# A gated feed-forward in which each pair of a gate block and an up block is made with seven block products, on one core of a Trainium2

## The reference

```python
def swiglu(x, w_gate, w_up, w_down):
    return (jax.nn.silu(x @ w_gate) * (x @ w_up)) @ w_down

    h = h + 0.5 * swiglu(rmsnorm(h, ffn1_norm[i]), ffn1_w_gate[i], ffn1_w_up[i], ffn1_w_down[i])
    ...
    h = h + 0.5 * swiglu(rmsnorm(h, ffn2_norm[i]), ffn2_w_gate[i], ffn2_w_up[i], ffn2_w_down[i])
    gate = jax.nn.sigmoid(rmsnorm(h, ple_gate_norm[i]) @ ple_w_gate[i])
    emb = rmsnorm(p[i] @ ple_w_proj[i], ple_norm[i])
    h = h + gate * emb
```

## Time and profile before

| | us |
|---|---|
| median of 3 runs | 2253.64 |
| lowest, highest | 2253.39, 2257.74 |
| profiled execution | 2255.11 |
| its span, first to last instruction | 2253.3 |
| PE busy | 2224.9 |
| DVE busy | 1337.6 |
| ACT busy | 892.6 |
| POOL busy | 321.0 |

### The profile page before, as it was taken

How to read it: one execution, slowest core, us unless ns; L and a number is a source line. 1 busy time by engine, 2 the same in 40 slices (tenths; PEclk the granted TensorE clock), 3 DMA queues, 4 the chain that set the end, 5 groups by cost and what they waited for, 6 DMA issues and landing times.

```text
span 2253.3 us, 30491 instructions
## 1 busy us (share of the span) xinstructions
PE 2224.9 (99%) x12660; PEld 1855.0 (82%) x12667; DVE 1337.6 (59%) x1562; ACT 892.6 (40%) x1190; POOL 321.0 (14%) x191
## 2 busy tenths in 40 slices
PE   9999999999999999999999999999999999999999
PEld 7888888878888888888886789899876858898998
DVE  6434446597644345475557675576567874855754
ACT  4222234345422332353238543344434574533532
POOL 2000001030100100021002123123100301231230
PEclk9999999999999999999999999999999999999999
DMA  5233322320233323232320133333333201334332
GB/s 190 94 94 94 111 75 86 101 72 20 84 99 107 93 94 93 76 111 94 113 75 20 55 107 111 122 112 104 99 115 80 72 20 45 115 112 122 106 110 94
DMA packets 201186, 208.12 MB, mean 92 GB/s; under 512 B 7042, under 2 KB 195218, under 8 KB 201076
## 3 DMA queue, kind: packets, MB, share of 16 engines
q1 hardware_dynamic: 201076, 206.56, 29.6%
...
## 4 chain that ended last, share of the span: by engine, by line
PE 91%; DVE 6%; ACT 2%; issue 1%; DMA 0%; SPq 0%; ACTq 0%; DVEq 0%
PE psum L867 78%; PE psum L957 4%; PE psum L955 4%; PE psum L956 4%; DVE sm L2880 1%; DVE w_lo L404 1%; DVE rstd L2287 0%; PE psum L1409 0%; PE psum L1401 0%; DVE free_x L2269 0%; ACT w_hi L391 0%; ACT free_h L1685 0%; DVE free_h L2272 0%; DVE free_x L3002 0%; DVE sm L3000 0%
## 5 line engine op out<-in xcount | busy, mean ns | idle before, releaser
L867 PE MATMUL psum<-xg_lo,w_hi 128*128 128x512 f32 (+1 forms) x1576 | 608.5, 389 | 0.4 <-ACT free_x L1685 0.4
L867 PE MATMUL psum<-xg_hi,w_hi 128*128 128x512 f32 (+1 forms) x1528 | 596.2, 390 | 3.9 <-DVE xg_lo L2269 1.7
L867 PE MATMUL psum<-xg_hi,w_lo 128*128 128x512 f32 (+1 forms) x1528 | 592.9, 388 | 0.0
L391 ACT ACTIVATE w_hi<-w_raw 128x2048 fp32r<-128x2048 f32 (+1 forms) x148 | 281.6, 1903 | 382.9 <-PE psum L867 363.3
L404 DVE TENSOR_TENSOR w_lo<-w_raw,w_hi 128x2048 fp32r<-128x2048 f32 (+1 forms) x146 | 340.9, 2335 | 151.2 <-ACT w_hi L391 148.0
L867 PEld LDWEIGHTS psum<-xg_lo,w_hi 128*128 128x128 f32 x1576 | 295.6, 188 | 62.2 <-ACT free_x L1685 1.4
L867 PEld LDWEIGHTS psum<-xg_hi,w_hi 128*128 128x128 f32 x1528 | 287.0, 188 | 68.0 <-issue 4.9
L867 PEld LDWEIGHTS psum<-xg_hi,w_lo 128*128 128x128 f32 x1528 | 286.9, 188 | 59.5
L867 PE MATMUL psum<-h_hi,w_hi 128*128 128x512 f32 x696 | 278.1, 400 | 3.1 <-DVE w_lo L404 2.8
L867 PE MATMUL psum<-h_hi,w_lo 128*128 128x512 f32 x696 | 271.8, 391 | 0.0
L867 PE MATMUL psum<-h_lo,w_hi 128*128 128x512 f32 x696 | 271.8, 390 | 0.0
...
## 6 DMA issues: line engine op xcount, KB each, us to landing
...
```

Source lines behind the costliest of these rows:

```text
L391: e.activation(w_hi[:, wside(c), 0:n], w_raw[:, c % 2, 0:n], ACT.Copy).then_inc(sem("hi_done"), 1)
L867: return pe.matmul(out, lhsT, rhs, start=start, stop=stop)
```

## The change

The gated feed-forwards join `FAST`. ffn1 keeps two plain pairs at its start, ffn2 one (`PLAIN`); the other 2 + 4 + 3 and 3 + 4 + 3 pairs, 19 in all, are made by `fast_up` on PE and by a new function `fast_gated` on ACT and DVE, with a gate block and an up block as the two weight blocks. POOL's sums are written out for them too. The activation sums of ffn1 are made between its plain pairs, through the buffer `trig` (the sine and cosine tables, which are not in use yet); those of ffn2 are made in wout1, as wout2 does for mlp0. The constants move up in the larger `arena`, the embedding input and its split move into `buf_a`, `buf_b`, `buf_c` and `ssq`, its load comes later, its result moves, its sum and root go into `trig`. In the second group of ffn2 the load of `w_third` waits for the sum of the embedding's squares, since both use `sq`. The scratch memory for GpSimd's own DMAs, which the kernel does not issue, shrinks to make room. The core of the diff:

```diff
-FAST = ("mlp0", "mlp1")
+FAST = ('ffn1', 'ffn2', 'mlp0', 'mlp1')
+PLAIN = {"ffn1": 2, "ffn2": 1, "mlp0": 1, "mlp1": 1}
+STAGE = {"ffn1": 0, "ffn2": 2, "mlp0": 5, "mlp1": 7}
 def plan():
...
         sq = alias("sq", [P, 2, S], F32, 4 * KB + 2 * S * 4)
         rs_hi = alias("rs_hi", [P, S], F32R, 4 * KB + S * 4)
         rs_part = nc.alloc_sbuf_tensor_at("rs_part", [P, 2, P], F32R, offset=buf_d_at)
...
-                first, n_pairs = at[name, g, "up"] + (2 if g == 0 else 0), tiles // per - (g == 0)
+                plain_pairs = PLAIN[name] if g == 0 else 0
+                first, n_pairs = at[name, g, "up"] + 2 * plain_pairs, tiles // per - plain_pairs
+                group_first[name, g] = first
+                if n_pairs % 2:
+                    odd_turn[first] = len(odd_turn)
...
-        X_WITH = {"wout2": ((), (0, 1), (2,), ()), "wout3": ((0,), (1,), (2,), ())}
-
...
+        X_WITH = {"wout1": ((), (0, 1), (2,), ()), "wout2": ((), (0, 1), (2,), ()), "wout3": ((0,), (1,), (2,), ())}
...
+        def x_raw(p, i):
+
+            return trig if p == 0 else (buf_a, buf_c)[i % 2]
...
+
+            def load_p(buffer_free):
+
+                sp.wait_ge(sem("ms"), 3)
+                sp.dma_start(pos_int, io["positions_2"]).then_inc(sem("p_in"), 16)
+                sp.wait_ge(*buffer_free)
+                sp.dma_start(p_raw[:], io["p"].rearrange("(k p) t -> p k t", p=P)).then_inc(sem("p_in"), 16)
...
-                        sp.wait_ge(sem("ssq_done"), 7 * (p + 1))
+                        sp.wait_ge(*(third_free or (sem("ssq_done"), 7 * (p + 1))))
...
+                    if wg is not None and name in FAST:
...
+                        fast_loads(group_first[name, g], p, lambda q: (vu[:, :, (q + ahead) * BC:(q + ahead + 1) * BC],
+                                                                       vg[:, :, (q + ahead) * BC:(q + ahead + 1) * BC]),
+                                   (sem("emb_ssq"), 7) if (name, g) == ("ffn2", 1) else None)
...
+                            if (name, g, i) == ("ffn2", 0, 1):
+                                load_p((sem("u_read"), fast_groups[c0][-1] + 1))
...
-                        fast_up(c + 2 if g == 0 else c, p)
+                        for j in range(1, PLAIN[name] if g == 0 else 0):
+                            blk(c + 2 * j, a=xg(p))
+                            blk(c + 2 * j + 1, a=xg(p))
+                        fast_up(group_first[name, g], p)
...
+                def silu(q):
+                    if q >= 0:
+                        act.wait_ge(sem("gate_scaled"), made[q] + 1)
+                        a(buf_a[:], buf_a[:], ACT.Silu).then_inc(sem("silu"), 1)
+
+                def hidden_hi(q):
+                    if q < 0:
+                        if ahead:
+                            of_plain()
+                        return
+                    t = 2 * (q + ahead)
+                    act.wait_ge(sem("hmul"), h0 + q + 1)
+                    a(hidden(p)[0][:, t:t + 2, :], buf_b[:], ACT.Copy).then_inc(sem("h_hi_done"), 1)
...
+                for q in range(len(made)):
+                    split(7 * q + 3)
+                    silu(q - 1)
+                    copy(q, 0)
+                    split(7 * q + 4)
+                    hidden_hi(q - 1)
+                    copy(q, 1)
+                    split(7 * q + 5)
+                    copy(q, 2)
+                    for n in range(6, 10):
+                        split(7 * q + n)
+                q = len(made) - 1
+                hi(act, after)
+                silu(q)
+                hidden_hi(q)
+                hi(act, after + 1)
...
+                        for j in range(last):
+                            gated_pair(j, first=True)
...
+                            if p == 0:
+                                for i in range(2):
+                                    x_scale(p, i)
+                                    x_high(p, i)
+                                hi(act, c0)
+                            act.wait_ge(sem("evac"), c0 - 1)
+                            a(buf_c[:], buf_a[:], ACT.Silu).then_inc(sem("silu"), 1)
+                            if p == 0:
+                                for i in range(2, 4):
+                                    x_scale(p, i)
+                                    x_high(p, i)
...
+                def last_quarter(q):
+                    if q >= 0:
+                        dve.wait_ge(*strip_mark("pe", c0, 7 * q + 6))
+                        tt(buf_b[:, :, TS:S], by_halves(pair_banks(c0, q)[0]), scale[:, :, TS:S], ALU.mult).then_inc(sem("evac"), 1)
+
+                def gate_up(q):
+                    if q >= 0:
+                        dve.wait_ge(sem("evac"), c0 + 2 * q + 2)
+                        dve.wait_ge(sem("silu"), s0 + q + 1)
+                        tt(buf_b[:], buf_b[:], buf_a[:], ALU.mult).then_inc(sem("hmul"), 1)
...
+                for q, pair in enumerate(made):
+                    run, side_sum, first_sum = pair_banks(c0, q)
+                    last_quarter(q - 1)
+                    split(7 * q + 3)
+                    gate_up(q - 1)
+                    split(7 * q + 4)
+                    hidden_lo(q - 1)
+                    split(7 * q + 5)
+                    split(7 * q + 6)
+                    dve.wait_ge(*strip_mark("pe", c0, 7 * q + 3))
+                    dve.wait_ge(sem("h_done"), h0 + q)
+                    tt(buf_b[:, :, 0:TS], by_halves(first_sum), scale[:, :, 0:TS], ALU.mult)
+                    split(7 * q + 7)
+                    dve.wait_ge(*strip_mark("pe", c0, 7 * q + 4))
+                    tt(buf_a[:, :, TS:S], by_halves(run), by_halves(buf_c[:, q % 2, :]), ALU.add).then_inc(sem("u_read"), 1)
+                    split(7 * q + 8)
...
+                    dve.wait_ge(*strip_mark("pe", c0, 7 * q + 5))
+                    tt(buf_a[:, :, 0:TS], by_halves(side_sum), by_halves(buf_d[:, q % 2, :]), ALU.add).then_inc(sem("evac"), 1)
...
+                    dve.wait_ge(sem("u_read"), pair + 1)
+                    dve.wait_ge(sem("evac"), c0 + 2 * q + 1)
+                    stt(buf_a[:], buf_a[:], -1.0, scale, ALU.mult, ALU.mult).then_inc(sem("gate_scaled"), 1)
+                    split(7 * q + 9)
+                q = len(made) - 1
+                last_quarter(q)
+                gate_up(q)
+                hidden_lo(q)
                 lo(dve, after + 1)
...
+                                    x_split(p, i)
+                                    x_low(p, i)
+                            evac_scaled(c0 - 2, buf_a)
...
+                            if p == 0:
+                                lo(dve, c0)
+                                for i in range(2, 4):
+                                    x_split(p, i)
+                                    x_low(p, i)
+                            evac_scaled(c0 - 1, buf_b)
+                            dve.wait_ge(sem("evac"), c0)
+                            dve.wait_ge(sem("silu"), s0 + ahead)
+                            tt(buf_d[:], buf_b[:], buf_c[:], ALU.mult).then_inc(sem("hmul"), 1)
...
...
                     dve.wait_ge(sem("p_in"), 32)
-                    dve.tensor_copy(pos_row, arena[0:1, 1024:1536].bitcast(I32)).then_inc(sem("pos_f32"), 1)
+                    dve.tensor_copy(pos_row, pos_int).then_inc(sem("pos_f32"), 1)
...
+            def other_sums(c0):
+
+                made = fast_groups[c0]
+                for q, pair in enumerate(made):
+                    c = c0 + 2 * q
+                    pool.wait_ge(sem("w22_in"), 16 * (pair + 1))
+                    pool.wait_ge(*strip_mark("lo", c0, 7 * q + 1))
+                    add_rows(w_run[run_half[pair]], raw22(c0, q), sem("w_next"))
+                    pool.wait_ge(sem("w21_third_in"), 16 * (pair + 1))
+                    add_rows(w_third, raw22(c0, q), sem("w_third"))
+                    if q + 1 < len(made):
+                        first_sum(c0, q + 1)
+                    pool.wait_ge(sem(f"landed{(c + 1) % 2}"), 16 * ((c + 1) // 2 + 1))
+                    pool.wait_ge(*strip_mark("lo", c0, 7 * q + 2))
+                    add_rows(w_run[run_half[pair]], raw(c + 1, 0), sem("w_next"))
+
+            def fast_sums(name, with_first=None):
+
+                for g in range(len(GROUPS[name]) if name in FAST else 0):
+                    c0 = group_first[name, g]
+                    first_sum(c0, 0)
+                    if with_first and g == 1:
+                        with_first()
+                    other_sums(c0)
...
+            fast_sums("ffn1")
...
+            fast_sums("ffn2", lambda: add_squares("emb_sq", "emb_ssq", 0, 0, emb_sum))
...
     arrays, io = {}, {}
     given = {name: np.ascontiguousarray(inputs[name]) for name in INPUTS if name not in GAIN_ROWS}
     given["x"] = np.ascontiguousarray(inputs["x"].reshape(S, D).T)
```

188 lines of the change are left out of this document (121 added, 67 removed).

## The result

The changed kernel takes 2281.8 us (median of 4 runs, 2279.22 to 2282.46) against 2255.05 for the kernel before beside it: ratio 1.0116, interval 1.0102 to 1.0130, slower by 26.7 us. The prediction was 2270, range 2243 to 2287.

A forecast was written before the change was run, and what follows sets the result against it. PE's pace was taken to bound the kernel; -34.7 + 18.5 + 3 + 9.9 + 7.9 + 4.2 + 7.5 = +16.3 on the profiled 2255.11 gives 2271.4. That execution lies 1.5 above the median, so the forecast is 2270, range 2243 to 2287.

The forecast's parts named there:

- The gain: On PE, 19 fast pairs at 19.945 instead of 21.77 us each: 34.7 us less.
- The waits of the middle pairs: Seven gated fast pairs with one before and behind: PE waits 2.3 us each before product 4, for ACT's third copy.
- The last pairs: Last fast pair of each of six gated groups: one POOL sum less, the same chain 0.4 us late each.
- rival 3: Middle pairs wait, but one long start wait is absent: about 2262, or 2250 with both gone; chance 0.10, nearer 2250.
- The clock: PE falls to 1.2 GHz after waits near 3 us, 1.4 us each; two of seven middle pairs: 3, between 0 and 10.
- Rival 4: PE's clock falls after each of the seven waits and longer ones at the starts: 2277 to 2287; chance 0.15.
- ffn2's third group: Start of that group in ffn2: no wait or loss foreseen, 0 us.
- ffn1's first group: PE waits at product 1 for activation sums on DVE: 9.9 us with clock, between 3.4 and 12.
- ffn1's third group: First psum copy stands behind sine and cosine on ACT, so product 2 waits 6.5 us, plus 1.4 of clock: 7.9.
- ffn2's start: Activation sums in wout1 delay DVE's split for the feed-forward's first block: PE waits 2.77 us, clock 1.4, together 4.2.
- ffn2's second group: Strip 2's load queues behind strip 4's, which waits for the embedding's last addition: 6.1 us at product 2, 7.5 with clock.
- Rival 1: POOL gives way in middle pairs and narrow activation sums pass: middle pairs cost 2.4 us in all, 2244; chance 0.13.

The follow-up runs named there:

- e12: Changed kernel with all mends together, and POOL's weight sums cut to 256 of 1024 columns (rest left out of the computation): 2220.9 us, ratio 0.9857.
- e1: Changed kernel, but in gated fast pairs after each group's first, ACT rounds the previous hidden tiles after the psum copies and DVE splits them after strip 5: 2261.7 us.
- e2: Changed kernel, but POOL makes the next pair's first sum after the sum for strip 6 instead of before it: 2282.4 us, ratio 1.0121.
- e10: Changed kernel, but embedding squares go through buf_d, strip 4's load no longer waits for them, and POOL sums strip 2 before adding them: 2277.2 us.
- e4: Changed kernel, but ACT takes sine and cosine after the third psum copy of the third group's first pair, not ahead of the first: 2273.1 us.
- e5: Changed kernel, but ffn1 keeps three plain pairs and its activation sums are made one pair earlier: 2271.2 us, ratio 1.0066.
- e7: Changed kernel, but in ffn2's second group SP issues strip 3's load before the one waiting for the squares, and POOL sums strip 2 before adding them: 2282.1 us.
- e6: Changed kernel, but ffn2's activation sums are spread over wout1 one piece a block, instead of two in the second block: 2279.0 us.

## Why the prediction was right, and where it fell short

**The gain** was right. The first pair of ffn1's second group takes 19.93 (149.48 to 169.41 above), and e12 shows the gain whole when nobody is late: 33.2 us under the kernel before, for 18 x 1.825 = 32.9.

**The waits of the middle pairs** were right in place, cause and size: 2.3 forecast, 2.05 to 2.09 measured in six and 3.02 in one, by the chain as written: POOL twice, DVE's split and product held, ACT's rounding, two copies. In the pair shown the third copy ended 13.6 after the pair's start, forecast 13.7. e1 takes the chain away, e2 shows that the two sums count and not their order. The last pairs: 2.0 for 2.4. (The lower bound of this term is 7 x 1.0 + 6 x 0.4 = 9.4 and not 9.6, and rival 3 with both start waits gone is 2270 - 7.9 - 7.5 = 2255 by its own terms and not 2250; neither moves the forecast.)

**The clock** is the term that was mis-sized, and it makes nearly all of the difference between +16.3 and +26.7. For the middle pairs I took 3 us, falls in two of seven, because the one row had a wait of 2.77 and these were 2.3. It fell in six of seven at 1.6 each, 9.6, just under the upper bound of 10 that I had kept. For the first group's start I took 0.9; the clock had a mean of 0.57 over 12 us there, and the pair lost 2.3 beyond its idle time. In all the forecast had 42.9 of waits and 8.1 of clock; the trace has 41.0 of waits, 17.6 of clock and 2.8 of losses of some tenths. Rival 4, falls behind each wait and 2277 to 2287, came nearest: 2281.8 lies in its range and outside the forecast's own of 2258 to 2277. That the waits agree within 2 us in total is partly luck, since 1.6 at ffn2's third group that I had not seen and 1.3 too much at its second cancel.

**ffn1's first group** had 9.7 of idle time at product 1 for 8.2. Narrow steps are held like wide ones. One hold of 2.2 at 39.29, beside POOL's first sum, moved the 50.9 to 52.8, and behind it three steps were held, by 2.2, 2.2 and 1.4, where I had two holds of 2.4. The rule of the Trainium skill that I had weighed ("SBUF — State Buffer", section "SBUF: two separate sides"), a lock for the whole instruction of the other engine, agrees with this trace: 2.58 for 0.42, and 2.62 for 0.41 in e10. The price of the nearest wide rows was the right one to take, and the 3.4 for narrow steps that slip through was not.

**ffn1's third group, ffn2's start and its second group** came within 1.0 us each, the second group of ffn2 with a wait of 4.8 for 6.1 and 1.8 of clock for 1.4, ffn1's third with 6.25 for 6.5 and 2.5 for 1.4. e4 and e5 show the named cause in ffn1's two groups by taking it away. In ffn2's second group the named steps, the load behind the squares and ACT's first copy behind strips 2 and 3, were late as written, but e7 and e10 show that behind them others were late too; at ffn2's start e6 took away only part.

**ffn2's third group** I put at no cost, and it cost 1.8. The angles there were to be ready just in time; POOL held them, and the split behind them was late. Holds belonged into that step as into the others.

**Rival 1** fell: POOL did not give way, its first sum was on its way when DVE's split of strip 3 began. But my reading ended at the first late step. That DVE has no room in a middle pair in any order of ACT's list could have been worked out from the new list and the prices of the earlier trace rows: ten wide steps of 1.14 and four from psum of 0.6 are 13.8 of own work, and up to four holds of 1.9 make it 21.4 against a pace of 19.95.
